# Modulation products in four column groups of the array, with a small product that sums the quadrants

## The reference, cut to what matters

```
c_act = silu(c)                                   # (1, 1024)
mod   = c_act @ ada_w + ada_b                     # (1, 1024) @ (1024, 6144)
sh1, sc1, g1, sh2, sc2, g2 = split(mod, 6)
h = rmsnorm(x, norm_mix_w) * (1 + sc1) + sh1      # feeds proj = h @ w_in
x = x + g1 * mix(h)
h = rmsnorm(x, norm_mlp_w) * (1 + sc2) + sh2      # feeds the MLP
x = x + g2 * mlp(h)
```

## Time and profile before

| | |
|---|---|
| Median of 3 runs | 1412.34 us (1410.88 to 1412.73) |
| Span of the profiled execution | 1405.2 us |
| Median less span | 7.1 us |
| PE / DVE / POOL / ACT busy | 85% / 52% / 58% / 37% of the span |

### The profile page before, as it was taken

One profiled execution on the slowest core, in us unless ns is written; L12 is line 12 of the kernel. 1 busy time (PEld: TensorE's weight loads), 2 busy tenths in 40 slices (PEclk: granted clock), 3 DMA queues, 4 the chain that ended last, 5 costly groups with the idle time before them and its releaser, 6 DMA issues.

```text
span 1405.2 us, 18835 instructions
## 1 busy us (share of the span) xinstructions
PE 1200.8 (85%) x8000; PEld 1104.7 (79%) x8000; DVE 727.2 (52%) x778; ACT 521.1 (37%) x672; POOL 813.5 (58%) x225
## 2 busy tenths in 40 slices
PE   6699769576999996975779999976999788999976
PEld 5699658466998885973679999866987488999866
DVE  2396999656999005336555553074022536555054
ACT  1453210433343333456433333333554433333341
POOL 0476896133877882740157878844743146888863
PEclk9899879868999997997799999988999889999998
DMA  9442218412444554330034455524432033455540
GB/s 363 167 175 90 91 36 302 172 44 106 164 167 174 185 183 161 139 129 1 31 120 150 181 180 182 207 92 165 181 120 90 0 120 130 191 186 184 181 148 30
DMA packets 28131, 200.95 MB, mean 143 GB/s; under 512 B 3089, under 2 KB 3473, under 8 KB 4881
## 3 DMA queue, kind: packets, MB, share of 16 engines
q1 hardware_dynamic: 26624, 190.30, 37.0%
q10 hardware_dynamic: 1424, 9.46, 1.8%
HBM read 198.70 MB, written 1.05 MB: 142 GB/s over the span
## 4 chain that ended last, share of the span: by engine, by line
PE 68%; DVE 20%; ACT 5%; issue 4%; DMA 1%; POOL 1%; DVEq 0%; ACTq 0%; POOLq 0%
PE bank L491 19%; PE bank L496 18%; PE bank L497 18%; PE bank L569 6%; DVE hT_hi L1344 4%; DVE hT_lo L1345 3%; DVE arena L1677 2%; PE bank L620 2%; DVE hid_lo L1679 2%; DVE arena L1529 1%; PE bank L613 1%; DVE hid_hi L1678 1%; PE bank L857 1%; PE bank L856 1%; POOL w_lo L1279 1%
## 5 line engine op out<-in xcount | busy, mean ns | idle before, releaser
L1279 POOL TENSOR_TENSOR w_lo<-raw,w_hi 128x2048 fp32r<-128x2048 f32 (+1 forms) x159 | 731.3, 4600 | 569.6 <-PE bank L491 489.2
L949 ACT ACTIVATE w_hi<-raw 128x2048 fp32r<-128x2048 f32 (+1 forms) x159 | 299.6, 1886 | 342.1 <-PE bank L491 288.2
L491 PE MATMUL bank<-hT_hi,w_hi 128*128 128x256 f32 (+1 forms) x1360 | 392.1, 288 | 35.1 <-DVE hT_lo L1345 30.1
L496 PE MATMUL bank<-hT_lo,w_hi 128*128 128x256 f32 (+1 forms) x1360 | 389.3, 286 | 0.0
L497 PE MATMUL bank<-hT_hi,w_lo 128*128 128x256 f32 (+1 forms) x1360 | 389.1, 286 | 0.0
L491 PEld LDWEIGHTS bank<-hT_hi,w_hi 128*128 128x128 f32 (+1 forms) x1360 | 264.3, 194 | 39.7 <-DVE hT_lo L1345 20.3
L496 PEld LDWEIGHTS bank<-hT_lo,w_hi 128*128 128x128 f32 (+1 forms) x1360 | 264.2, 194 | 0.2
L497 PEld LDWEIGHTS bank<-hT_hi,w_lo 128*128 128x128 f32 (+1 forms) x1360 | 263.7, 194 | 0.3
L491 PE MATMUL bank<-w_hi,hT_hi 128*128 128x256 f32 (+2 forms) x544 | 164.5, 302 | 35.0 <-DVE hT_lo L1345 29.0
L496 PE MATMUL bank<-w_lo,hT_hi 128*128 128x256 f32 (+2 forms) x544 | 161.8, 298 | 0.0
L497 PE MATMUL bank<-w_hi,hT_lo 128*128 128x256 f32 (+2 forms) x544 | 161.7, 297 | 0.0
(11 more groups left out here) (242 smaller groups left out, 1347.0 us busy)
## 6 DMA issues: line engine op xcount, KB each, us to landing
raw<-wstream SPq DMA_DIRECT2D x179, 1024.0 KB, 4.8
arena<-prow ACTq DMA_DIRECT2D x2, 2560.0 KB, 8.9
x_res<-x ACTq DMA_DIRECT2D x1, 1024.0 KB, 12.4
rows<-prow ACTq DMA_DIRECT2D x2, 512.0 KB, 15.4
out<-x_res SPq DMA_DIRECT2D x1, 1024.0 KB, 4.0
const_sb<-const ACTq DMA_DIRECT2D x1, 936.0 KB, 14.2
raw<-wstream SPq DMA_DIRECT2D x1, 768.0 KB, 4.1
raw<-wstream SPq DMA_DIRECT2D x1, 544.0 KB, 3.6
```

Of the source, the lines that this page charges most:

```text
L491: ins = mm(o, a[0], b[0], start=start, stop=False)
L496: mm(o, a[0], b[1], start=False, stop=False)
L949: A(w_hi[n % HI][:, 0:m], raw[:, slot % RAW, 0:m], ACT.Copy).then_inc(weights_rounded, 1)
L1279: nc.gpsimd.tensor_tensor(w_lo[n % LO][:, 0:m], raw[:, slot % RAW, 0:m], w_hi[n % HI][:, 0:m].bitcast(F32), ALU.subtract).then_inc(weights ...
```

## The change

Each product's stationary operand is 32 columns wide instead of 128, and its output goes to 32 rows of the bank. Chunk k goes to quadrant k modulo 4, so a quadrant accumulates two chunks, and the four quadrants of a bank hold four partial sums, each repeated in 32 rows. DVE copies the bank to SBUF (`modulation_part`, into `lev_tmp`), and PE multiplies the copy by `pick_row`, which is 1 in one row of each quadrant and 0 elsewhere (`modulation_sum`, a new entry `ms` of the plan, with a bank of its own). For a gate row that is one product of 512 columns. For columns it is four products with 128 columns of the copy as the stationary operand and one moving column, so the result comes out as columns and DVE only adds the bias.

On PE, the sum of unit u stands behind the products of unit u+1, and it waits (`in_sbuf`) until DVE has copied unit u. On DVE, the reading of sum u-1 stands behind the copy of unit u. `pick_row` is set by five more memsets at the start.

```diff
-    plan = [("mod", u) for u in range(4)]
+    def modulations(first, end):
+        for u in range(first, end + 1):
+            if u < end:
+                plan.append(("mod", u))
+            if u > first:
+                plan.append(("ms", u - 1))
+    modulations(0, 4)
...
-    plan.extend([("mod", u) for u in range(4, N_ADA // 2)])
+    modulations(4, N_ADA // 2)
...
-                    for k in range(DC):
-                        last = mm(b[:, j * T:(j + 1) * T], csil[:, k:k + 1].to_broadcast([P, P]), w[:, k, :],
-                                  start=k == 0, stop=k == DC - 1)
+                    for half in range(2):
+                        for g in range(4):
+                            k = 4 * half + g
+                            last = mm(b[32 * g:32 * g + 32, j * T:(j + 1) * T],
+                                      csil[:, k:k + 1].to_broadcast([P, 32]), w[:, k, :],
+                                      start=half == 0, stop=half == 1)
                     last.then_inc(psum_full if j else ada_used, 1)
+            def modulation_sum(u):
+                in_sbuf("mod", u)
+                b = begin("ms", u)
+                part = lev_tmp[u % 2]
+                if u in (4, 5, 10, 11):
+                    last = mm(b[:, :], pick_row, part, start=True, stop=True)
+                else:
+                    for c in range(4):
+                        last = mm(b[:, c:c + 1], part[:, c * P:(c + 1) * P], pick_row[:, 0:1],
+                                  start=True, stop=True)
+                last.then_inc(psum_full, 1)
+            def modulations(first, end):
+                for u in range(first, end + 1):
+                    if u < end:
+                        modulation(u)
+                    if u > first:
+                        modulation_sum(u - 1)
...
+            def modulation_part(u):
+                b = wait_full("mod", u)
+                done(V.tensor_copy(lev_tmp[u % 2], b[:, :]), "mod", u)
             def modulation_columns(u):
-                b = wait_full("mod", u)
-                done(V.tensor_tensor(h4(lev_tmp[u % 2]), h4(b[:, :]), ident.unsqueeze(1).to_broadcast([P, 4, P]),
-                                     ALU.mult), "mod", u)
-                m = mod[:, 4 * u:4 * u + 4]
-                link(V.tensor_reduce(m, h4(lev_tmp[u % 2]), AX.X, ALU.add))
-                link(V.tensor_tensor(m, m, col("ada_b", 4 * u, 4), ALU.add))
+                b = wait_full("ms", u)
+                done(V.tensor_tensor(mod[:, 4 * u:4 * u + 4], b[:, 0:4], col("ada_b", 4 * u, 4), ALU.add), "ms", u)
             def modulation_row(u, row):
-                b = wait_full("mod", u)
-                done(V.tensor_tensor(row, b[:, :], row, ALU.add), "mod", u)
+                b = wait_full("ms", u)
+                done(V.tensor_tensor(row, b[:, :], row, ALU.add), "ms", u)
...
             dve.wait_ge(gate_bias_loaded, 32)
-            modulation_row(4, rows[:, 1, 0:512])
-            modulation_row(5, rows[:, 1, 512:1024])
-            for u in range(6, 10):
-                modulation_columns(u)
-            modulation_row(10, g2_row[:, 0:512])
-            modulation_row(11, g2_row[:, 512:1024])
+            gate_rows = {4: rows[:, 1, 0:512], 5: rows[:, 1, 512:1024], 10: g2_row[:, 0:512], 11: g2_row[:, 512:1024]}
+            for u in range(4, 13):
+                if u < 12:
+                    modulation_part(u)
+                if u > 4 and u - 1 in gate_rows:
+                    modulation_row(u - 1, gate_rows[u - 1])
+                elif u > 4:
+                    modulation_columns(u - 1)
+            wait_done("ms", 9)
```

More of the change, by code:

```diff
@@ L163, in psum_plan @@
 def psum_plan():
-    plan = [("mod", u) for u in range(4)]
+    plan = []
+    def modulations(first, end):
[5 more added lines that the diff above has]
+    modulations(0, 4)
     def transposes(stage):
@@ L353, in build @@
         assert g2_at + D <= ARENA
+        pick_row = arena[:, g2_at + D:g2_at + D + P]
+        assert g2_at + D + P <= ARENA
         act_out, product = unit_logits[0:2], unit_logits[2:4]
@@ L636, in _ @@
             pe.wait_ge(c_ready, 1)
-            for u in range(4):
-                modulation(u)
+            modulations(0, 4)
             pe.wait_ge(const_loaded, 16)
@@ L673, in _ @@
                     last.then_inc(psum_full, 1)
-            for u in range(4, N_ADA // 2):
-                modulation(u)
+            modulations(4, N_ADA // 2)
             pe.wait_ge(levels_summed, 1)
@@ L1437, in _ @@
             V.memset(hpad, 0.0)
+            link(V.memset(pick_row, 0.0))
+            for g in range(4):
+                V.memset(pick_row[32 * g:32 * g + 1, :], 1.0)
             link(V.memset(ones[:, :], 1.0))
@@ L1452, in _ @@
             dve.wait_ge(const_loaded, 16)
-            for u in range(4):
-                modulation_columns(u)
+            for u in range(5):
+                if u < 4:
+                    modulation_part(u)
+                if u:
+                    modulation_columns(u - 1)
+            wait_done("ms", 3)
             V.scalar_tensor_tensor(out=norm_a, in0=mod[:, 8:16], scalar=1.0, in1=col("mix_w", 0, 8),
```

## The result

| | before | after |
|---|---|---|
| Median | 1412.5 us (1410.9 to 1413.7, 4 runs) | 1435.5 us (1428.3 to 1437.6, 4 runs) |
| Ratio | | 1.0159, 95% interval 1.0132 to 1.0185 |
| Span of the profiled execution | 1405.2 us | 1435.8 us |
| PE busy | 85% | 82% |

The change costs 22.5 us (18.6 to 26.1). The forecast was 1427 with a range of 1415 to 1452. The two spans differ by more, 30.6 us. Where a run has both a time and a span, the time is 1.8 to 1.9 us the longer (1437.6 against 1435.8 for the profiled run of the changed kernel). So of the 7.1 us between the span and the median of before, less than 2 lie around the span, and the rest says that the profiled execution was a short one of its kernel. The changed kernel's profiled run was the longest of its four. So sizes are taken from the timed ratios here, and places from the traces.

The account below looks back on a forecast made before the run. It took the first group as bound by loads, then PE, and the second by DVE's selection. 1405.2 - 5.5 + 20 = 1419.7 us of span, plus 7.1 between span and median, gave 1427 us, range 1415 to 1452.

Parts of the forecast that it names:

- the forecast's own 1417 to 1437: Whole kernel: from gain 6.5, loss 18.6 and 7 of slack downstream, to gain 3, loss 24 and a lasting half clock.
- What bounds the kernel: Units 0 to 3: loads first, PE only in the second half; units 4 to 11: DVE's key selection until 243.7 us.
- The column groups are parallel: Modulation products: four column groups run side by side, a tile taking 0.9 us at full clock, 1.7 at half.
- "take turns" rival: Both groups: column groups run one after another, 3.51 us a tile, +43 us in all, 1455 us; chance 0.18.
- The 2.6 times: Attention scores on PE: fp32 products in four row groups overlap 2.6 times, the nearest evidence for parallel column groups.
- Sum 4 waits for the selection, nine loads move behind it: Second group: PE stops after four tiles until DVE copies unit 4; ada15 to ada23 load afterwards, `hgo` read 20 us later.
- The pace of the loads: Second group after the selection: loads taken at 2.6 us a tile, from a span of 2.46 to 3.0.
- over 350: Sign of being right: nine loads after the selection's end, back to back at over 350 GB/s.
- the other bound: Load pace from landing times: 3.0 us a tile, which makes the second group's loss 24 us.
- The first group: Units 0 to 3: faster products leave loads to set the pace, ada7 landing at 33.1 us; gain 5.5 us (3 to 6.5).
- The sum: Whole kernel: 5.5 us gained in units 0 to 3 and 20 lost in units 4 to 11, +14.5.
- Nothing gives it back: Downstream of the second group: norm, convolution, attention and output GEMM wait for one another, so the 20 us loss stays.

Follow-up runs that it names:

- filler: Changed kernel with three full-width products of 256 columns, their result overwritten, ahead of every wait for a modulation tile: 1430.3 us, ratio 1.0152.
- sums-last kernel: Changed kernel with the eight sums of the second group moved behind all its products: 1404.0 us, ratio 0.9972 to the kernel before.
- the shorter sums: Changed kernel with one product instead of four in each column sum of the second group: 1430.6 us, ratio 1.0152 to the kernel before.
- column groups undone: Changed kernel's order, copies and sums, but with products of 128 columns: 1443.7 us, ratio 1.0240 to the kernel before.

## Why the prediction was right, point by point

- *Time and range.* The measured 1435.5 us lies in the range, and 1.5 us inside the upper end of the forecast's own 1417 to 1437. The mechanism is the one forecast; its size was at the edge.
- *What bounds the kernel.* Right: loads first in the first group, DVE's selection in the second, although the chain of waits shows PE there for 54 us. The 8.48 us that the chain of the earlier trace rows puts down to a load are no gap of PE: its timeline has it idle for 1.65 us there.
- *The column groups are parallel.* Right: 1.07 us a tile at the full clock, 1.93 at half (0.9 and 1.7 were taken). The "take turns" rival falls. The 2.6 times that I read for the row groups set a stretch at a clock of 0.50 against one at 0.58, so it was somewhat low. By the rule of the Trainium skill (TensorEngine Tiling (Array Packing), Theoretical Speedup) it could be up to four times as fast; the trace agrees, with 3.51 / 1.07 = 3.3.
- *Sum 4 waits for the selection, nine loads move behind it.* Right, and shown three ways: 37.05 us of idle PE in the trace, the loss gone when only the order is changed, and +29 us when only the wait is added to the kernel before. Sum 4 took 2.07 us (1.7 taken), ada15 was there at 252.40 (252.8 taken).
- *The pace of the loads.* This is the term that was mis-sized. I took 2.6 us a tile, near the 2.46 of the first 25 us. From ada15's start to ada23's, 252.40 to 279.84, it is 3.43, and in the repeat of the changed kernel 3.1; the windows' 340 to 348 GB/s give 3.0 to 3.1, against the "over 350" that was to show the forecast right. With the other bound, 3.0, the sum had +24 for this group, close to the +26 of the trace and above the +21.1 (18 to 24) timed for that group alone.
- *The first group.* The gain of 5.5 us was too large: 1.6 in the trace (under the 3 to 6.5 given), 3.8 (1.3 to 6.3) timed. Three terms failed. The first is the load: ada7's products started at 35.14 and not at 33.1. The pace of all loads was as taken (5.01 MB in 11.9 us, 421 GB/s), but I had counted ACT's own loads as nearly landed by 23.25 us, and 1.09 MB of them were still to come: weight loads that are issued sooner share the engines with them. All seven profiled executions with column groups in the first group and no filler have 1.05 to 1.10 MB there, the four with full-width products there 0.04 to 0.16. The second is the clock: it was at 0.50 from 17 us on, so those products took 1.94 instead of 0.9 and a sum 1.76 instead of 1.0. The third is the order: I left out that sum 2 stands between them and sum 3, 1.8 us more, of which DVE's copy hides 0.7.
- *The sum.* Timed +22.5 against +14.5 forecast. Both misses go in one direction: in the second group the faster end was taken for the loads, in the first ACT's share of them, the half clock and sum 2 were missed.
- *Nothing gives it back.* Right: DVE's shift is 26.3 us at 275 us of before and 27 near 600 us. It grows to 30.5 us by the end, mostly near 700 and 1110 us of before, which the timed difference doesn't show. In the second profile of the changed kernel it goes the other way, from 24 at 300 us to 22.6 at the end. What follows ACT's reading of `hgo` lasts 1142 to 1150 us in all twelve profiled executions, in no order with the change, and 1149 and 1142 in the two of the changed kernel. So that growth is spread between executions; its cause stays open.

What stays open: why a tile takes 3.0 us here, when the loads of the first 25 us ran at a pace of 2.5. In the sums-last kernel the same loads ran at 370 GB/s (2.8 us) under the selection. Two windows of the changed kernel (columns as in rows 6) show that the pace is not even:

```profile
255.00:260.00 5.00, 2.83 (x28) 1.12 (x32) 0.00 (x0) 0.00 (x0) 0.00 (x0) 0.53 1.07 431
260.00:265.00 5.00, 4.70 (x36) 2.53 (x28) 0.85 (x2) 0.00 (x0) 0.00 (x0) 0.50 0.87 297
```

The loads reach 431 GB/s where PE waits for them and fall to 297 where PE is at work on a tile, a sum and a tile and lets the buffers go late. That points at the ring of three buffers. It is not shown: the shorter sums alone and the full clock with filler left the mean where it was, and no run had both at once.

## What to carry to other kernels

Before a faster product, look for what is queued behind its consumer. A copy to another engine in the middle of PE's order ties PE, and through it the loads, to everything that stands ahead of the copy on that engine; put the dependent product behind all independent ones, or give the copy to an engine that is idle. When loads take over as the bound, price them by their slower measured pace, not by the best stretch, and count which other queue still shares the engines once they are issued sooner.

## What the runs showed of the hardware

- fp32 products of 256 columns in four column groups, all writing one bank, run side by side: 16 instructions in 1.07 us at the full clock against 3.51 in the full array, 3.3 times as fast.
- A fp32 product with 128 stationary columns and one moving column costs as much as one with 128 moving columns: four in 0.95 us at the full clock (column groups undone), 0.24 us each as in the earlier trace rows, and 0.47 at a granted clock of 0.50.
- The granted clock was mostly 0.50 where the narrow products waited for loads, with PE idle for 0.4 to 2.3 us at a time between them in the second group; filler products lifted it to 1.00, and the time moved by less than can be told.
- Weight loads issued sooner slowed the loads of another queue: ACT's 512 KB load of `pT` landed 29.6 us after its issue instead of 20.9.
